# Expert stage of a two-block transformer layer: two experts side by side in the gate/up products, the sums read straight from the banks, gathers ahead in quarters, 13 ring slots

## The chip, the cores and the metric

The kernel runs on one core of a Trainium2 chip. The metric is the time of one execution on the device in microseconds (us), here as the median of several runs. The engines are named as in the profile: PE (TensorE, matrix products; PEld is its weight load), DVE (VectorE), ACT (ScalarE), POOL (GpSimd) and SP (SyncE, which here issues nearly all transfers). They run side by side and wait for one another by semaphores.

## What is computed

The reference is two transformer blocks one after the other on 512 tokens of width 1024, all in float32: a first block with a gated linear recurrence, attention and a dense feed-forward part, then a second one with three attention branches and a feed-forward part of 16 experts. The change touches the last part only:

```python
def expert_choice_ffn(x, w_router, w_gate_up, w_down):     # x (1, 512, 1024)
    cap = EC_CAPACITY_FACTOR * T // N_EXPERTS              # 64 tokens for each of 16 experts
    aff = jax.nn.softmax(x @ w_router, axis=-1)
    gate, idx = lax.top_k(jnp.swapaxes(aff, 1, 2), cap)
    xs = x[bidx, idx]                                      # (16, 64, 1024)
    h = jnp.einsum('becd,edf->becf', xs, w_gate_up)        # (16, 64, 2048)
    hg, hu = jnp.split(h, 2, axis=-1)
    ye = jnp.einsum('becf,efd->becd', jax.nn.silu(hg) * hu, w_down)
    ye = ye * gate[..., None]
    return jnp.zeros_like(x).at[bidx, idx].add(ye)
# then: layer_norm(DN_ALPHA * x + ffn, ln2_g, ln2_b)
```

The gate/up weights of an expert are 1024 x 2048 numbers (8.4 MB), its down weights 1024 x 1024 (4.2 MB), 201 MB for all sixteen. Each is used once.

## The kernel before

Everything ahead of the expert stage is a list of steps (`plan`) that each engine walks through in its own program; it is the same before and after and ends at about 1133 us. Then come `experts_sp`, `experts_pool`, `experts_act`, `experts_dve` and `experts_pe`, one function for each engine. They compute router logits, softmax and the 64 best tokens of each expert (to about 1158 us), and from there on the experts.

**Order.** Experts go in fours (`QUADS`). An item of `todo` is `("G", x)`, the gate/up products of expert x, or `("D", g)`, the down products of the pair g (experts 2g and 2g+1). The order of one quad is D of the quad before, G, G, G, D, G; in the last one it is D5, G12, G13, G14, G15, D6, D7. Every item has 8 chunks of weights, 1 MB each (128 partitions x 8 KB), 192 in all. A chunk of G holds 128 of the 1024 rows of the expert's gate/up matrix; in D, even and odd chunks belong to the two experts of the pair.

**Ring.** SP loads the chunks in order (`load`, L724). 11 tiles RING of 8 KB per partition are reused in turn (`RS`, L132). Five chunks (5, 6, 7, 13, 14) go to tiles ONCE in two halves, and those tiles aren't used again for weights. So 16 chunks are loaded ahead. Each later load waits (`slot_free`, L748) until PE has counted the chunk that held the slot as used; PE counts two chunks after each pair (`used`, L1190).

**Gate/up** (`gate_up`, L1178). The 64 tokens of an expert fill only half of the 128 columns of PE's array. So two products run in the two halves at once: the lower half takes the even chunk of a pair (a 128-row slice of the sum), the upper half the odd one, both of the same expert. After 8 chunks the four banks GU hold two partial sums, one in partitions 0 to 63, the other in 64 to 127. ACT copies the upper ones to LOH (L831), DVE adds them to the lower ones into GUS (L976), ACT makes Silu of the gate half into SG (L835), DVE multiplies (L980). PE may start the next expert in a bank only when DVE has added it (`ev`). `hidden` (L1146) turns the 64 x 1024 result with 8 transposes into one bank, and ACT copies it to HT.

**Down** (`down`, L1192). Here the two halves of the array take the two experts of a pair: sums in partitions 0 to 63 and 64 to 127 of the banks YB. ACT and DVE weight them and split them into a high and a low part (YHM, YLM). `scatter` (L1117) adds them to the tokens: 8 products with a 0/1 matrix SS, 3, 3 and 2 of them behind the first pairs of the item after D, and DVE adds each to X (L970).

**Gather** (`gather`, L1090). Before each quad PE forms the tokens of its four experts with 0/1 matrices OHT, 64 matmuls, into the four banks XG, two of which are gate/up banks. ACT scales them into the one tile XS (L822). The gather runs in one piece after the quad's last G; `columns` (each slot's token number and weight) and `hidden` follow at once.

**End.** During D6 and D7, `residual` and `late_scatter` (L1131, L1136) put X and the contribution of pair 6 into the banks; pair 7 follows, then the layer norm and the output. During G13 `spread_rows` (L1157) spreads the norm's gains over the partitions.

Of the kernel before, what the change touches and what calls it, by code (L numbers as in the profile page):

```python
# [33 lines left out]
RS = 11  # L34
# [51 lines left out]
def build(nc, x, w_in, w_out, w_ffn_in, w_ffn_out, mem, w_in2, w_memkv, w_branch, w_out2, w_router,  # L86
# [7 lines left out]
    def sem(name):  # L94
# [37 lines left out]
    RING = [at(f"RING{i}", kb, [P, 2048]) for i, kb in enumerate((*(R0 + 8 * i for i in range(8)), 181.5, 189.5, 16))]  # L132
    ONCE = {n: [at(f"ONCE{n}{h}", kb, [P, 1024]) for h, kb in enumerate(kbs)]
            for n, kbs in ((5, (52, 32)), (6, (36, 40)), (7, (44, 48)), (13, (56, 60)), (14, (197.5, 201.5)))}
# [45 lines left out]
    XS = at("XS", 8, [P, KT, QE, CAP])  # L180
    SS = at("SS", 24, [P, 2, S], F32R)
    HT = at("HT", 28, [P, 2, 2, KT, CAP])
    GUS = at("GUS", 36, [CAP, 4 * 512])
    LOH = at("LOH", 44, [CAP, 4 * 512])
    SG = at("SG", 52, [CAP, DFE])
    YHM = at("YHM", 56, [P, D], F32R)
    YLM = at("YLM", 197.5, [P, D], F32R)
    YH7 = at("YH7", 36, [P, D], F32R)
    YL7 = at("YL7", 40, [P, D], F32R)
    JUNK = at("JUNK", 44, [P, 4, 512])  # L190
# [488 lines left out]
    def tokens_first(st, f, bank, dst):  # L679
# [9 lines left out]
    (used, oht, ssr, gth, xsc, ev_lo, ev, su, hm, tp, hc, yh, yl, sct, acc) = (  # L689
        sem(n) for n in "used oht ssr gth xsc ev_lo ev su hm tp hc yh yl sct acc".split())  # L690
# [4 lines left out]
    HB = TR[0]  # L695
# [24 lines left out]
    def experts_sp(sp):  # L720
# [3 lines left out]
        def load(n):  # L724
            kind, x = todo[n // 8]
            c, r = n % 8, ring_place(n)
            if kind == "G":
                src = gu_v[:, 8 * x + c, :]
            else:
                src = dn_v[:, (2 * x + c % 2) * 4 + c // 2, :]  # L730
            if r is not None:
                sp.dma_start(RING[r % RS][:, :], src).then_inc(ring_in[r % RS], 16)
                return
            for h in range(2):
                if n == 5 and h:
# [38 lines left out]
    def experts_act(act, chain):  # L774
# [43 lines left out]
        def tokens(p):  # L818

            for d in range(KT):  # L820
                act.wait_ge(gth, 4 * p + d // 2 + 1)
                A(XS[:, d, :, :], XG[d // 2][:, d % 2 * 256:d % 2 * 256 + 256].rearrange(  # L822
                    "p (e c) -> p e c", e=QE), ACT.Identity, scale=LNC[:, 0, d:d + 1],
                  bias=LNC[:, 1, d:d + 1]).then_inc(xsc, 1)

        def gated(x):

            if x:
                act.wait_ge(ev, 4 * x)
# [3 lines left out]
            if x:  # L833
                act.wait_ge(tp, x)
            A(SG[:, :], GUS[:, 0:DFE], ACT.Silu).then_inc(su, 1)  # L835

        def hidden(x):

            act.wait_ge(tp, x + 1)
            if x == 0:  # L840
                wait(act, "xal", total)
            A(HT[:, x // 2 % 2, x % 2, :, :], HB[:, :].rearrange("p (f c) -> p f c", c=CAP), ACT.Copy).then_inc(hc, 1)

        tokens(0)
        for idx, (kind, x) in enumerate(todo):
            if idx == len(todo) - 1:
                act.preload_act_table_set("sqrt_and_others")
            else:
                act.wait_ge(used, 8 * idx + 8)
            if kind == "D":  # L850
                outputs(x)
                continue
            gated(x)
            if x % QE == QE - 1 and x < E - 1:
                tokens(x // QE + 1)
            if x == E - QE:
                rows_spread(0)
            hidden(x)
            if x == E - QE:
                for q in range(1, 4):  # L860
                    rows_spread(q)

# [29 lines left out]
    def experts_dve(dve, chain):  # L892
# [79 lines left out]
        def gated(x):  # L972
# [15 lines left out]
        for idx, (kind, x) in enumerate(todo):  # L988
            if kind == "G":
                gated(x)  # L990
                if x % QE == QE - 1 and x < E - 1:
                    slot_columns(x // QE + 1)
                if x % QE == 0 and x < E - QE:
                    dve.wait_ge(gth, x + 4)
                    one_hot_tokens(x // QE + 1)
# [39 lines left out]
    def experts_pe(pe):  # L1035
# [54 lines left out]
        def gather(p, evicted):  # L1090

            pe.wait_ge(oht, 2 * p + 1)
            if p:
# [1098 lines left out]
```

## Time and profile before

| | |
|---|---|
| median of 3 runs | 1653.49 us (1651.95 to 1653.94) |
| the profiled execution's own time | 1654.13 us |
| its span, first to last instruction | 1652.3 us |
| mean granted clock of PE over the span | 0.977 |
| busy over the span: PE, DVE, ACT, POOL | 94%, 42%, 32%, 8% |
| share of PE in the chain that ended last | 87% |
| weights' transfers in the expert stage, RING (1 MB each) | 123 of gate/up, 62 of down |

How it is read: the page gives busy time by engine, a strip of 40 slices of 41.3 us each, and the costliest groups of instructions by line. The other views are answers on the trace: the waits (who waited for whom, summed), the chain of waits (followed back from the last instruction to what released each step), the timeline, the groups by line and form, and windows. A line of the windows has: stretch, its length in us, busy us (and number of instructions) of PE, PEld, DVE, ACT and POOL, then the granted clock of PE (1.00 is full speed), the busy share of the DMA engines and the GB/s that they moved. Times are us from the span's start. A float32 matmul leaves two records, so 8 matmul calls are 16 records. "L1208 x32" in the chain is a run of 32 records of that line.

### The profile page before, as it was taken

To read this page: it belongs to the slowest core of one execution; us is meant where nothing else is said; L and a number is where in the kernel's file an instruction comes from. 1 tells how busy PE (TensorE), PEld (TensorE's weight loads), DVE (VectorE), ACT (ScalarE), POOL (GpSimd) and SP (SyncE) were. 2 spreads that over 40 slices of the span, in tenths; PEclk is the share of its full clock that TensorE was granted. 3 is DMA by queue.
4 is the path that set the end of the run, shared out by engine and by line. 5 is a ranking of instruction groups with operands and counts; after the bars stand their busy time and mean duration, and the time that the engine had idled before them with its cause. 6 is when DMAs were issued, how large, how long until landed. Compare 5 with 4: busy or idle time off the path is not lost.

```text
span 1652.3 us, 20133 instructions
## 1 busy us (share of the span) xinstructions
PE 1549.1 (94%) x7883; PEld 1085.7 (66%) x7883; DVE 701.3 (42%) x1053; ACT 531.7 (32%) x862; POOL 138.5 (8%) x186
## 2 busy tenths in 40 slices
PE   7999899999999999999999999996999999989996
PEld 6788668888888888887677678775535334334332
DVE  6565755343334335664435343366222322222223
ACT  5634534222222214234444433233222112112222
POOL 3000000000000001143102110002500000000001
PEclk9999899999999999999999999998999999999998
DMA  6221223333323327233112112429699999999993
GB/s 209 83 96 53 76 64 100 84 98 102 102 99 94 89 77 215 79 110 95 39 38 66 39 54 92 135 77 392 251 401 397 422 421 420 421 421 421 421 421 155
DMA packets 137067, 306.93 MB, mean 186 GB/s; under 512 B 7480, under 2 KB 97472, under 8 KB 113296
## 3 DMA queue, kind: packets, MB, share of 16 engines
q1 hardware_dynamic: 132608, 294.99, 47.7%
q0 software_dynamic: 3792, 10.15, 2.1%
q8 instruction: 66, 1.08, 0.3%
q10 hardware_dynamic: 576, 0.50, 0.1%
q14 instruction: 25, 0.20, 0.0%
HBM read 299.32 MB, written 4.56 MB: 184 GB/s over the span
## 4 chain that ended last, share of the span: by engine, by line
PE 87%; DVE 5%; DMA 3%; ACT 2%; issue 2%; SPq 0%; ACTq 0%; DVEq 0%
PE bank L1188 13%; PE bank L1965 12%; PE bank L1967 12%; PE bank L1966 12%; PE bank L1208 6%; PE bank L1973 4%; PE bank L1974 4%; PE bank L1975 4%; PE bank L2014 3%; PE bank L2115 2%; PE bank L2130 2%; DMA RING<-w_down 2%; PE bank L1984 2%; PE bank L1986 2%; PE bank L1985 2%
## 5 line engine op out<-in xcount | busy, mean ns | idle before, releaser
L1965 PE MATMUL bank<-XH,WH 128*128 128x512 f32 x768 | 303.5, 395 | 5.1 <-DVE XL L1795 2.0
L1967 PE MATMUL bank<-XH,WL 128*128 128x512 f32 x768 | 300.1, 391 | 0.0
L1966 PE MATMUL bank<-XL,WH 128*128 128x512 f32 x768 | 300.0, 391 | 0.0
L1616 DVE TENSOR_TENSOR WL<-RAW,WH 128x2048 fp32r<-128x2048 f32 (+1 forms) x90 | 191.8, 2131 | 142.4 <-ACT WH L1416 142.4
L1188 PE MATMUL bank<-RING,XS 128*64 128x512 f32 x496 | 224.9, 602 | 16.8 <-DVE GUS L976 14.2
L1189 PE MATMUL bank<-RING,XS 128*64 128x512 f32 x488 | 221.7, 603 | 0.0
L1416 ACT ACTIVATE WH<-RAW 128x2048 fp32r<-128x2048 f32 (+1 forms) x90 | 160.0, 1778 | 143.9 <-PE bank L1975 117.9
L1965 PEld LDWEIGHTS bank<-XH,WH 128*128 128x128 f32 x768 | 144.9, 189 | 38.4 <-issue 7.5
L1967 PEld LDWEIGHTS bank<-XH,WL 128*128 128x128 f32 x768 | 144.9, 189 | 30.7
L1966 PEld LDWEIGHTS bank<-XL,WH 128*128 128x128 f32 x768 | 145.0, 189 | 29.5 <-issue 0.2
L1188 PEld LDWEIGHTS bank<-RING,XS 128*64 128x64 f32 x496 | 65.2, 138 | 150.4 <-issue 144.8
L1208 PE MATMUL bank<-RING,HT 128*64 128x512 f32 x512 | 118.4, 614 | 6.4 <-DMA RING<-w_down 3.4
L976 DVE TENSOR_TENSOR GUS<-bank,LOH 64x512 f32<-64x512 f32 x64 | 39.6, 675 | 151.6 <-ACT LOH L831 151.6
L1208 PEld LDWEIGHTS bank<-RING,HT 128*64 128x64 f32 x512 | 39.3, 141 | 77.8 <-issue 77.6
L831 ACT ACTIVATE LOH<-bank 64x512 f32<-64x512 f32 x64 | 32.8, 590 | 178.7 <-PE bank L1189 178.6
L1973 PE MATMUL bank<-WH,AH 128*128 128x512 f32 x176 | 68.5, 389 | 1.0 <-issue 1.0
L1975 PE MATMUL bank<-WH,AL 128*128 128x512 f32 x176 | 68.5, 389 | 0.0
L1974 PE MATMUL bank<-WL,AH 128*128 128x512 f32 x176 | 68.5, 389 | 0.0
L1387 POOL TENSOR_SCALAR PB<-PB,ST 128x256 f32<-128x256 f32 (+1 forms) x80 | 46.7, 596 | 248.8 <-DVE ST L1741 248.5
L1631 DVE TENSOR_TENSOR FP<-bank,FG 128x512 f32<-128x512 f32 x22 | 15.2, 691 | 121.7 <-PE bank L1967 121.7
L1189 PEld LDWEIGHTS bank<-RING,XS 128*64 128x64 f32 x488 | 64.2, 138 | 0.0
L1984 PE MATMUL bank<-WH,XH 128*128 128x256 f32 x224 | 63.8, 285 | 0.2 <-ACT SE L1459 0.2
(360 smaller groups left out, 2411.4 us busy)
## 6 DMA issues: line engine op xcount, KB each, us to landing
RING<-w_gu SPq DMA_DIRECT2D x123, 1024.0 KB, 14.5
RING<-w_down SPq DMA_DIRECT2D x62, 1024.0 KB, 17.0
RAW<-w_in SPq DMA_DIRECT2D x66, 512.0 KB, 4.7
RAW<-w_ffn_in SPq DMA_DIRECT2D x44, 512.0 KB, 4.6
RAW<-w_ffn_out SPq DMA_DIRECT2D x20, 512.0 KB, 4.3
RAW<-w_out SPq DMA_DIRECT2D x16, 512.0 KB, 4.4
RAW<-w_branch SPq DMA_DIRECT2D x24, 256.0 KB, 2.9
ONCE<-w_gu SPq DMA_DIRECT2D x10, 512.0 KB, 19.7
```

The source lines that it names most:

```text
L1188: T.matmul(GU[b][0:CAP, :], XS[:, c - 1, e, :], weight(n - 1, 512 * b), start=c == 1, stop=c == 7)
L1189: ins = T.matmul(GU[b][CAP:P, :], XS[:, c, e, :], weight(n, 512 * b), start=c == 1, stop=c == 7)
L1208: ins = T.matmul(YB[g][h][e * CAP:e * CAP + CAP, :], HT[:, g % 2, e, 2 * r + k, :], weight(n - 1 + e, D * k + 512 * h), start=r == 0 and k ...
L1416: A(WH[:, u % 2, :n], RAW[:, u % 2, :n], ACT.Copy).then_inc(s["w_hi"], 1)
L1616: V.tensor_tensor(WL[:, u % 2, :n], RAW[:, u % 2, :n], WH[:, u % 2, :n].bitcast(F32), ALU.subtract).then_inc(s["w_lo"], 1)
L1965: T.matmul(bank[:, :st.nt], wh[:, k, c], hi, start=k == 0, stop=False)
L1966: T.matmul(bank[:, :st.nt], wh[:, k, c], lo, start=False, stop=False)
L1967: ins = T.matmul(bank[:, :st.nt], wl[:, k, c], hi, start=False, stop=k == st.K - 1)
L1973: T.matmul(bank[:, :], hi, wh[:, k, :], start=k == 0, stop=False)
L1974: T.matmul(bank[:, :], hi, wl[:, k, :], start=False, stop=False)
L1975: ins = T.matmul(bank[:, :], lo, wh[:, k, :], start=False, stop=k == st.K - 1)
L1984: T.matmul(o, XHs[:, k, t], wh[:, k, :], start=k == 0, stop=False)
```

## The change

Two experts of a pair now take the two halves of the array in G as well, so that an item `("G", g)` is a pair with 16 chunks, alternating between its experts, and the order is G0, G1, D0, G2, D1, ..., G7, D6, D7. Each bank then holds whole sums, of one expert in partitions 0 to 63 and of the other in 64 to 127. The copies to LOH and the adds into GUS fall away: ACT makes Silu from the gate banks (two instructions of 512 columns over 128 partitions), DVE multiplies with the up banks. `hidden` makes 8 transposes of 128 x 128 into two banks, once for a pair. The gather of quad p runs in four quarters ahead of chunks 6, 8, 10 and 12 of the item G(2p-1), through the two banks SB, into the other one of two XS tiles; `columns` goes to the end of D0, D2 and D4. `spread_rows` goes to the second half of G7. The ring has 13 slots, and three chunks (6, 11, 14) are loaded to ONCE tiles; it is 16 ahead in either case. The core of the diff:

```diff
-RS = 11
+RS = 13
-    RING = [... for i, kb in enumerate((*(R0 + 8 * i for i in range(8)), 181.5, 189.5, 16))]
+    RING = [... for i, kb in enumerate((*(R0 + 8 * i for i in range(8)), 181.5, 189.5, 197.5, 56, 16))]
-            for n, kbs in ((5, (52, 32)), (6, (36, 40)), (7, (44, 48)), (13, (56, 60)), (14, (197.5, 201.5)))}
+            for n, kbs in ((6, (36, 40)), (11, (44, 32)), (14, (48, 52)))}
...
-    todo = []
-    for p in range(QUADS):
-        a, b, c, d = (("G", QE * p + x) for x in range(QE))
-        before, here = ("D", 2 * p - 1), ("D", 2 * p)
-        todo += [before] * (p > 0) + ([a, b, c, d, here, ("D", 2 * p + 1)] if p == QUADS - 1 else [a, b, c, here, d])
-    chunks = 8 * len(todo)
+    todo = [("G", 0)]
+    for g in range(1, E // 2):
+        todo += [("G", g), ("D", g - 1)]
+    todo.append(("D", E // 2 - 1))
+    order = [(kind, g, c) for kind, g in todo for c in range(16 if kind == "G" else 8)]
+    chunks = len(order)
...
-                src = gu_v[:, 8 * x + c, :]
+                src = gu_v[:, 8 * (2 * g + c % 2) + c // 2, :]
...
-        for n in ringed[:-1]:
+        for n in ringed[:RS - 2]:
             load(n)
         wait(sp, "res", total)
-        for n in (ringed[-1], *sorted(ONCE, reverse=True)):
+        for n in (*ringed[RS - 2:], 6, 14, 11):
...
# ACT
-            for b in range(4):
-                A(LOH[:, 512 * b:512 * b + 512], GU[b][CAP:P, :], ACT.Copy).then_inc(ev_lo, 1)
-            act.wait_ge(ev, 4 * x + 2)
-            if x:
-                act.wait_ge(tp, x)
-            A(SG[:, :], GUS[:, 0:DFE], ACT.Silu).then_inc(su, 1)
+            act.wait_ge(used, 16 * g + 16 + 8 * max(g - 1, 0))
+            if g:
+                act.wait_ge(tp, 2 * g)
+            for h in range(2):
+                A(SG[:, 512 * h:512 * h + 512], GU[h][:, :], ACT.Silu).then_inc(su, 1)
...
# DVE
-            for b in range(4):
-                dve.wait_ge(ev_lo, 4 * x + b + 1)
-                V.tensor_tensor(GUS[:, 512 * b:512 * b + 512], GU[b][0:CAP, :],
-                                LOH[:, 512 * b:512 * b + 512], ALU.add).then_inc(ev, 1)
-            dve.wait_ge(su, x + 1)
-            dve.wait_ge(ev, 4 * x + 4)
-            V.tensor_tensor(SG[:, :], SG[:, :], GUS[:, DFE:], ALU.mult).then_inc(hm, 1)
+            for h in range(2):
+                dve.wait_ge(su, 2 * g + h + 1)
+                sg = SG[:, 512 * h:512 * h + 512]
+                V.tensor_tensor(sg, GU[2 + h][:, :], sg, ALU.mult).then_inc(hm, 1)
...
# PE
+            p, k, e = g // 2, c // 2, 2 * (g % 2)
             for b in range(4):
-                if c == 1 and x:
-                    pe.wait_ge(ev, 4 * (x - 1) + b + 1)
+                if c == 1 and g:
+                    if b < 2:
+                        pe.wait_ge(su, 2 * g + b - 1)
+                    else:
+                        pe.wait_ge(hm, 2 * g + b - 3)
...
-                T.matmul(GU[b][0:CAP, :], XS[:, c - 1, e, :], weight(n - 1, 512 * b), start=c == 1, stop=c == 7)
-                ins = T.matmul(GU[b][CAP:P, :], XS[:, c, e, :], weight(n, 512 * b), start=c == 1, stop=c == 7)
+                T.matmul(GU[b][0:CAP, :], XS[p % 2][:, k, e, :], weight(n - 1, 512 * b), start=k == 0, stop=k == KT - 1)
+                ins = T.matmul(GU[b][CAP:P, :], XS[p % 2][:, k, e + 1, :], weight(n, 512 * b),
+                               start=k == 0, stop=k == KT - 1)
...
+            if kind == "G" and x % 2 and x < LAST and c in (6, 8, 10, 12):
+                gather(x // 2 + 1, c // 2 - 3)
+            landed(n)
...
+                if prev and prev[0] == "G" and c == 3:
                     hidden(prev[1], 8 * scattered)
+                if kind == "D" and x % 2 == 0 and x < LAST - 1 and c == 7:
+                    pe.wait_ge(hc, 2 * x + 4)
+                    columns(x // 2 + 1, 8 * scattered)
+                if (kind, x) == ("G", LAST) and c > 8:
+                    spread_rows(c // 2 - 4)
...
-            if kind == "G" and x % QE == QE - 1 and x < E - 1:
-                gather(x // QE + 1, 4 * x + 4)
-                columns(x // QE + 1, 8 * scattered)
-                hidden(x, 8 * scattered)
-                made += 1
```

## Rows read from the trace of the kernel before

**Rows 1.** Page, part 2: GB/s moved, in 40 slices of the span.

```profile
GB/s 209 83 96 53 76 64 100 84 98 102 102 99 94 89 77 215 79 110 95 39 38 66 39 54 92 135 77 392 251 401 397 422 421 420 421 421 421 421 421 155
```

**Rows 2.** Windows of 20 us in the expert stage (columns as told above).

```profile
1160.00:1180.00 20.00, 20.00 (x117) 13.14 (x118) 0.61 (x4) 4.07 (x8) 9.23 (x5) 0.90 0.35 138
1180.00:1200.00 20.00, 18.43 (x91) 6.89 (x87) 7.94 (x7) 4.99 (x7) 13.34 (x6) 1.00 0.87 356
1200.00:1220.00 20.00, 18.50 (x89) 7.10 (x89) 5.80 (x9) 6.33 (x11) 0.00 (x0) 1.00 0.93 375
...
1260.00:1280.00 20.00, 19.16 (x89) 8.60 (x90) 1.99 (x7) 2.77 (x5) 0.00 (x0) 0.91 0.91 373
...
1460.00:1480.00 20.00, 16.78 (x74) 6.13 (x70) 4.68 (x7) 1.26 (x2) 0.00 (x0) 1.00 1.02 422
```

**Rows 3.** Waits of TensorE from 1150 us on: total us, times, longest us.

```profile
PE bank L1188 <- DVE GUS L976: 14.2, 9, 2.1
...
PE bank L1128 <- DVE X L970: 3.8, 12, 0.3
PE bank L1208 <- DMA RING<-w_down: 3.4, 3, 1.4
```

**Rows 4.** Waits of SyncE's DMA queue from 1050 us on, same columns.

```profile
SPq L732 <- PE bank L1189: 262.8, 63, 23.8
```

**Rows 5.** Timeline at the first gate/up products: start us, duration us, what.

```profile
1169.59 0.64 PE L1188 MATMUL bank<-RING,XS 128*64 128x512 f32 x1
...
1173.28 19.28 SPq L732 DMA_DIRECT2D RING<-w_gu  x8
```

**Rows 6.** The chain that ended last, expert stage: start us, us, what.

```profile
1134.27 2.61 PE bank L1042 x22
...
1217.22 6.87 PE bank L1208 x32
...
1225.28 7.02 PE bank L1208 x32
...
1251.98 0.32 PE bank L1102
...
1259.85 0.80 PE bank L1113 x8
...
1348.90 0.61 PE bank L1188
...
1354.74 0.57 PE bank L1188
...
1365.23 0.57 PE bank L1188
```

**Rows 7.** The same chain, from the last experts to the end.

```profile
1539.25 1.06 PE bank L1165 x4
...
1592.52 6.87 PE bank L1208 x32
...
1631.05 0.69 ACT YH L811
```

**Rows 8.** Windows of 2 us at the end of the weight transfers.

```profile
1618.00:1620.00 2.00, 2.00 (x11) 0.62 (x8) 0.00 (x0) 0.00 (x0) 0.00 (x0) 1.00 1.05 389
1620.00:1622.00 2.00, 2.00 (x6) 1.00 (x6) 0.00 (x0) 0.00 (x0) 0.00 (x0) 1.00 0.68 257
1622.00:1624.00 2.00, 2.00 (x12) 0.74 (x12) 0.00 (x0) 0.00 (x0) 0.00 (x0) 1.00 0.23 84
```

**Rows 9.** Windows of 8 us, for the granted clock beside the busy time.

```profile
1342.00:1350.00 8.00, 6.03 (x28) 1.98 (x26) 1.41 (x2) 1.26 (x2) 0.00 (x0) 1.00 1.01 417
1462.00:1470.00 8.00, 5.42 (x26) 2.01 (x26) 1.41 (x2) 1.26 (x2) 0.00 (x0) 1.00 1.01 419
1556.00:1564.00 8.00, 6.46 (x18) 2.21 (x20) 3.69 (x5) 3.06 (x6) 0.00 (x0) 0.57 1.02 423
```

**Rows 10.** Groups by line and form, ACT, from 1130 us on.

```profile
L831 ACT ACTIVATE LOH<-bank 64x512 f32<-64x512 f32 x64 | 32.8, 590 | 178.7 <-PE bank L1189 178.6
```

More of the change, by code:

```diff
@@ L688, in build @@
     row_ps, spread = sem("row_ps"), sem("spread")
-    (used, oht, ssr, gth, xsc, ev_lo, ev, su, hm, tp, hc, yh, yl, sct, acc) = (
-        sem(n) for n in "used oht ssr gth xsc ev_lo ev su hm tp hc yh yl sct acc".split())
+    (used, oht, ssr, gth, xsc, su, hm, tp, hc, yh, yl, sct, acc) = (
+        sem(n) for n in "used oht ssr gth xsc su hm tp hc yh yl sct acc".split())
     GU = [LIN[0], LIN[1], LIN[2], PV]
@@ L844, in experts_act @@
[L844 to L849, printed above, removed]
-            if kind == "D":
-                outputs(x)
-                continue
[L853 to L860, printed above, removed]
+                bank = (SB[d // 2 % 2] if p else XG[d // 2])[:, d % 2 * 256:d % 2 * 256 + 256]
@@ new lines, in tokens, with gated, hidden @@
+                A(XS[p % 2][:, d, :, :], bank.rearrange("p (e c) -> p e c", e=QE), ACT.Identity,
+                  scale=LNC[:, 0, d:d + 1], bias=LNC[:, 1, d:d + 1]).then_inc(xsc, 1)
+        def gated(g):
+            act.wait_ge(used, 16 * g + 16 + 8 * max(g - 1, 0))
[3 more added lines that the diff above has]
+                A(SG[:, 512 * h:512 * h + 512], GU[h][:, :], ACT.Silu).then_inc(su, 1)
+        def hidden(g):
+            if g == 0:
+                wait(act, "xal", total)
+            for i in range(2):
+                act.wait_ge(tp, 2 * g + i + 1)
+                A(HT[:, g % 2, 4 * i:4 * i + 4, :], TR[i][:, :].rearrange("p (f s) -> p f s", s=P),
+                  ACT.Copy).then_inc(hc, 1)
@@ L861, in experts_act @@
+        tokens(0, range(4))
+        for kind, g in todo:
+            if kind == "D":
+                if g == LAST:
+                    act.preload_act_table_set("sqrt_and_others")
+                else:
+                    act.wait_ge(used, 16 * g + 32 + 8 * g + 8)
+                outputs(g)
+                continue
+            if g % 2 and g < LAST:
+                tokens(g // 2 + 1, range(4))
+            if g == LAST:
+                for q in range(4):
                     rows_spread(q)
+            gated(g)
+            hidden(g)
@@ L990, in experts_dve @@
                 gated(x)
[L991 to L995, printed above, removed]
+                if x % 2 and x < LAST:
+                    slot_columns(x // 2 + 1)
+                if x % 2 == 0 and x < LAST - 1:
+                    dve.wait_ge(gth, 2 * x + 4)
+                    one_hot_tokens(x // 2 + 1)
             else:
@@ L1088, in experts_pe, with gather @@
         pe.wait_ge(s["x2l"], TT)
-        def gather(p, evicted):
-            pe.wait_ge(oht, 2 * p + 1)
-            if p:
-                pe.wait_ge(yl, 2 * (2 * p - 1))
-            for d in range(KT):
-                if p and d == 4:
-                    pe.wait_ge(ev, evicted)
-                o = XG[d // 2][:, d % 2 * 256:d % 2 * 256 + 256]
+        def gather(p, batch):
+            if batch == 0:
+                pe.wait_ge(oht, 2 * p + 1)
+                if p > 1:
+                    pe.wait_ge(yl, 2 * (2 * p - 2))
+            if p and batch >= 2:
+                pe.wait_ge(xsc, 8 * p + 2 * batch - 2)
+            for d in (2 * batch, 2 * batch + 1):
+                o = (SB[batch % 2] if p else XG[batch])[:, d % 2 * 256:d % 2 * 256 + 256]
                 for t in range(TT):
@@ L1124, in scatter @@
             if k == 1:
-                pe.wait_ge(s["colg"], min((g + 1) // 2 + 1, QUADS))
+                pe.wait_ge(s["colg"], min(g // 2 + 2, QUADS))
             if k >= 2:
@@ L1144, in late_scatter, with hidden @@
                     ins.then_inc(fsc, 1)
-        def hidden(x, scattered):
-            pe.wait_ge(hm, x + 1)
+        def hidden(g, scattered):
+            pe.wait_ge(hm, 2 * g + 2)
             if scattered:
                 pe.wait_ge(acc, scattered)
-            T.matmul(HB[:, 0:CAP], SG[:, 0:2 * P:2], ident[0:CAP, 0:CAP], start=True, stop=True)
-            for f in range(1, KT):
+            for f in range(KT):
                 c = slice(f // 2 * 2 * P + f % 2, f // 2 * 2 * P + 2 * P, 2)
-                ins = T.transpose(HB[:, CAP * f:CAP * f + CAP], SG[:, c], ident[0:CAP, 0:CAP])
-            ins.then_inc(tp, 1)
+                ins = T.transpose(TR[f // 4][:, f % 4 * P:f % 4 * P + P], SG[:, c], ident)
+                if f % 4 == 3:
+                    ins.then_inc(tp, 1)
         def spread_rows(q):
```

102 lines of the change are left out of this document (40 added, 62 removed).

## The prediction

> **What bounds the kernel now.** I read the page's row of GB/s first [rows 1]. The slices of 41.3 us from about 1200 us on stand at 397 and then at 420 to 422 GB/s for ten slices: a plateau. The change touches only the expert stage, and this is it: from slot choice (about 1158 us) to the end it streams 192 chunks of 1.0486 MB through the ring. The plateau says that the transfers, not the products, may set the pace. The windows then show where the stream is below it [rows 2]: 138, 356 and 375 GB/s in the first three windows and 373 at 1260 us, against 422 at 1460 us. In the latter, TensorE is busy 16.8 of 20 us.
>
> Next the waits. TensorE waits 14.2 us for the sums of the two bank halves, 3.8 us for residual sums, and only 3.4 us for weights [rows 3]. SyncE's queue in contrast waits 263 us for gate/up products to free a slot [rows 4]; but that costs nothing while earlier transfers are still in flight. So two resources run nearly level: a transfer stream of 192 chunks, and TensorE, a little behind it. The end shows which is late: the stream's rate falls from 389 to 257 to 84 GB/s in three windows of 2 us [rows 8], which is (389+257+84)/422 x 2 = 3.5 us of full rate after 1618, a nominal stream end of 1621.5 us. TensorE's last weight product ends 9.6 us after that, at 1631.05, where the tail begins [rows 7]. The tail (weighting, last scatter, layer norm, output) takes 1652.3 - 1631.05 = 21.2 us, and the change leaves it alone.
>
> **The unit of account.** One chunk at 422 GB/s [rows 2] is 1.0486/0.422 = 2.49 us, a pair 4.97 us. TensorE needs 6.87/2 = 3.44 us for a pair of down chunks [rows 6]. A gate/up pair has the same 8 matmul calls, and its first goes from 1169.59 to the slot's release at 1173.28 [rows 5]; I take 3.5 us for either. Other TensorE work: the hidden transposes of one expert 1225.28 - 1217.22 - 6.87 = 1.2 us; a gather 1259.85 - 1251.98 = 7.9 us; columns 0.8 us; eight scatters (1354.74 - 1348.90 - 3.5) + (1365.23 - 1354.74 - 7.0) = 5.8 us, their waits included [rows 6].
>
> **Part 1: products side by side, whole sums.** The number and shape of the gate/up matmuls stay, so their cost stays. What goes is, per expert, four ACT copies of 590 ns [rows 10], four adds on DVE, and TensorE's wait for them: 14.2 us in all [rows 3]. In their place one pair of experts waits for Silu and a multiply straight from the banks. Only after G0 does the next G follow at once: there the first Silu must finish before the banks are reused. No row shows a Silu of 512 columns from a bank; the copy of the same width is the nearest row, 0.59 us, so the wait is 0.6 us or so, and at most the present longest, 2.1 us [rows 3]. It falls into G1, where TensorE isn't late for anything. For all other g a down group of 14 us lies between. Value: 13 us of TensorE time. Queued behind ACT's new wait for 16 chunks are its weighted outputs; these come a group later, so nobody waits.
>
> **Part 2: transposes for two experts in one.** 16 x 1.2 us become 8 runs of 8 transposes, twice as wide. In this place the trace shows only narrow ones; a run lies between 1.2 us (width free) and 2.4 us (width pays fully). The nearest row of wide ones, 22 transposes of 128 x 128 in 2.61 us, has 0.12 us for each [rows 6], so I take 1.2: 10 us of TensorE saved; 0 is the other end. Their input (two Silus, two multiplies, 2 to 3 us) is asked for two pairs, 7 us, after the group's end: covered.
>
> **Part 3: gather ahead, in quarters, second XS.** 7.9 us stay, but now as four pieces of 2.0 us ahead of four pairs of an odd G. Before, gather, columns and transposes stood in a row and released no slot for 11 us.
>
> **Part 4: 13 ring slots and 3 once-used ones instead of 11 and 5.** 16 chunks are loaded ahead either way, so the stream's first pause (until 1173.28 plus about 1 us) stays. But used pairs now hand back 2,2,2,1,2,1,2,1 slots instead of 2,2,1,0,2,2,1,1. Before: five slots are back after three pairs, the stream has work until 1174.2 + 5 x 2.49 = 1186.6, and the next slots are freed by the fifth pair, at 1188.6 or later: it runs dry. After: seven slots, work until 1191.6, fifth pair done at 1187. Carried on pair by pair, (a chunk starts 1.1 us after its slot is free and its forerunner done), the new order keeps at least 1.5 us of work queued in G0 and 3.0 us in G1, its two tight places, so no dry spell.
>
> **Sum for the stream.** Lost before, against 422: 20 x (66+47+49)/422 = 7.7 us in the windows at 1180, 1200 and 1260 [rows 2]. All of it comes back: nominal end 1621.5 - 7.7 = 1613.8 us. (Flat 422 from 1174.2 on would give 1611.6; that is the early bound. The late bound is 1621.5, nothing regained.)
>
> **Is TensorE there in time?** Per 48 chunks it now needs 24 x 3.5 + 2 x 5.8 + 7.9 + 0.8 + 2 x 1.2 = 106.7 us, the stream 119.3. From 1169.6 its work up to G7 adds to some 345 us, 1515 us; the first pair of G7 can't have landed before 1174.2 + 146 x 2.49 = 1537. So TensorE catches up by the middle of the stage and then waits for weights, some 25 us in all: this is where the 23 us of parts 1 and 2 go. They bring no more than the stream lets through.
>
> **The end.** G7 needs 28 + 5.8 + 4 x 1.06 for spreading rows [rows 7] = 38.0 us against 39.8, its extras in front, so it may end 0 to 2 us late. D6 and D7 take 1631.05 - 1592.52 = 38.5 us as now [rows 7]. D6 starts when its first pair is there, the stream's end less 14 x 2.49 and plus 2 us for the spread of a landing: -32.8. So TensorE ends 5.7 to 7.7 us after the stream's nominal end. I take 7.7, as both extras lie on one side: 1613.8 + 7.7 = 1621.5, which is 9.5 us before today's 1631.05. Of this, 7.7 us are the stream's, 1.9 the lag's. The profiled execution's own time is 1654.13 (span 1652.3), 0.6 above the median; less 9.5 gives 1644.6 for it, and 1644.0 against the median. Forecast **1644.0 us**.
>
> **Rivals.** *More than forecast*: the lag shrinks to the least there is (2 us for landing, half a pair 1.7) and the stream ends at 1611.6: TensorE ends at 1615.3, total 1637.7. For it: TensorE has 13 us of slack per 48 chunks. Against: the extras sit in D6 and D7. Chance of under 1641: 0.09.
>
> *The dry spells stay*: with 2 to 3 us queued, any late release idles the stream, and gathers now stand among products. Then only the lag's 1.9 us are won: 1651.6, no change that could be told. For it: the two tight places. Against: from 1280 us on the stream has no dry spell even with 11 slots. Chance near that: 0.08; between: part of 1647.5 to 1650.2, 0.08.
>
> *Slower: the clock falls because TensorE now waits.* Before, the granted clock read 0.57 over 8 us after a stretch of small products and a wait [rows 9]: 3.4 us lost. If TensorE, waiting 1.5 us in 5, drops to 1.2 GHz again and again in G7, D6 and D7 (76.5 us of work on 79.6 us of stream, 3 us of slack), five such spells cost 17 - 3 = 14 us at the end where nothing regains them: 1658. It decides from four spells on; fewer only shrink the gain. Against it: the two stretches where TensorE already waits for weights show 6.03 and 5.42 busy us in 8, which is the duty I forecast, at a clock of 1.00 [rows 9]; and a slow TensorE is a busy one. Chance 0.07.
>
> [...]
>
> **How the numbers follow.** Forecast case 0.68 (1641 to 1647.5), more gain 0.09, between 0.08, dry spells 0.08, slower 0.07. A measurement of this kernel can tell about 0.2%, 3.3 us: faster means under 1650.2. Faster 0.85, same 0.08, slower 0.07. Range: from 1639.5 (half of the better case) to 1650.2 (the between case whole).
>
> **What would show it.** Right: the plateau from 1180 us on with no window under 415 GB/s; TensorE waiting 20 us or more for RING and almost none for banks; last weight product 8 us or less after the nominal stream end, that at 1614. Wrong: windows under 400 between 1180 and 1280, a clock under 1.00 in the last 80 us, or a TensorE that reaches G7 later than 1537.

## The result and the profile after

The changed kernel takes 1645.86 us (median of 5 runs, 1643.30 to 1646.51) against 1653.51 us: ratio 0.9948, 95% interval 0.9938 to 0.9959. That is 7.7 us or 0.5% faster. The forecast was 1644.0 us in a range of 1639.5 to 1650.2. The profiled execution took 1645.86 us, 8.3 less than the profiled one of before; its span is 1644.1 us. In the changed code the gate/up products are L1181 and L1182, the down products L1202, the loads L728.

The page's row of GB/s, which answers [rows 1]:

```profile
GB/s 210 80 100 52 78 64 87 94 102 103 97 83 102 102 77 192 81 131 79 57 26 73 45 52 77 128 103 323 285 421 421 422 421 421 421 421 421 421 421 170
```

Before, two slices at the head of the plateau read 401 and 397, and eight at 420 to 422 followed (the prediction names only the 397 and counts ten); now it stands at 421 from its first slice on. The windows of 20 us (columns as before) answer [rows 2]:

```profile
1160.00:1180.00 20.00, 20.00 (x116) 13.70 (x118) 0.99 (x5) 5.37 (x9) 8.38 (x4) 0.89 0.38 143
1180.00:1200.00 20.00, 19.21 (x92) 6.42 (x90) 1.05 (x2) 1.08 (x2) 12.77 (x7) 1.00 1.01 424
1200.00:1220.00 20.00, 20.00 (x110) 9.82 (x108) 1.44 (x3) 3.13 (x6) 0.00 (x0) 1.00 1.01 419
...
1260.00:1280.00 20.00, 19.68 (x88) 6.92 (x86) 3.27 (x5) 0.00 (x0) 0.00 (x0) 1.00 1.01 420
...
1380.00:1400.00 20.00, 16.05 (x74) 5.49 (x70) 0.00 (x0) 0.00 (x0) 0.00 (x0) 1.00 1.02 423
```

Where 356, 375 and 373 GB/s stood, there are 424, 419 and 420. The dry spells (stretches in which the stream has no free slot to fill) are gone, and in the window at 1380 us TensorE is busy only 16 of 20 us, at a granted clock of 1.00. TensorE's waits from 1150 us on (total, times, longest), which answer [rows 3]:

```profile
PE bank L1181 <- issue: 11.7, 11, 1.3
PE bank L1202 <- DMA RING<-w_down: 10.0, 12, 1.4
...
PE bank L1118 <- DVE X L963: 3.8, 12, 0.3
PE bank L1202 <- issue: 2.8, 3, 1.3
PE bank L1181 <- ACT SG L828: 0.8, 1, 0.8
PE bank L1181 <- DMA RING<-w_gu: 0.8, 3, 0.3
```

The 14.2 us of waiting for half sums are gone. One wait of 0.8 us for Silu stands in their place, the one between G0 and G1. There are now about 25 us of idle time in front of products whose weights are not there: 10.0 and 0.8 us are put down to the transfers, and 11.7 and 2.8 us to "issue", which are pieces of the same length (up to 1.3 us, where a pair of products takes 3.5 and a pair of chunks 5.0). That these last 14.5 us are waits for weights too is read from their length and place; pe_late below bears it out. Not all of it is new: the kernel before has 3.4 us put down to transfers and, in front of gate/up products, 2.5 us to "issue".

Windows of 2 us at the end of the stream, which answer [rows 8]:

```profile
1606.00:1608.00 2.00, 2.00 (x12) 0.75 (x8) 0.00 (x0) 0.00 (x0) 0.00 (x0) 1.00 1.03 430
1608.00:1610.00 2.00, 2.00 (x10) 0.70 (x12) 0.00 (x0) 0.00 (x0) 0.00 (x0) 1.00 0.98 390
1610.00:1612.00 2.00, 2.00 (x9) 0.58 (x6) 0.00 (x0) 0.00 (x0) 0.00 (x0) 1.00 1.02 383
1612.00:1614.00 2.00, 2.00 (x7) 1.14 (x6) 0.00 (x0) 0.00 (x0) 0.00 (x0) 1.00 0.96 353
1614.00:1616.00 2.00, 2.00 (x10) 0.63 (x10) 0.00 (x0) 0.00 (x0) 0.00 (x0) 1.00 0.54 208
1616.00:1618.00 2.00, 2.00 (x11) 0.50 (x7) 0.00 (x0) 0.00 (x0) 0.00 (x0) 1.00 0.10 38
```

From 1608 us on this is (390+383+353+208+38)/422 x 2 = 6.5 us of full rate, a nominal end of 1614.5 us. Counted in the same way from 1614 us on, where its rate begins to fall (416 and 382 GB/s, then the three rows of [rows 8]), the kernel before ends at 1621.2 us and not at the prediction's 1621.5. The chain that ended last, which answers [rows 7]:

```profile
1566.09 25.99 DMA RING<-w_down
1592.08 0.14 issue
1592.22 3.65 PE bank L1202 x16
1595.87 1.91 PE bank L1124 x4
1597.79 3.58 PE bank L1202 x16
...
1622.76 0.70 ACT YH L807
```

The chain runs through a transfer up to 1592.08 us, the third pair of D6. From there on TensorE doesn't wait for weights any more, and 30.5 us of its own work stand before the tail. In the kernel before this stretch is much longer. The last piece of its chain in which TensorE waits for weights is

```profile
1467.18 1.28 issue
```

and from 1468.46 us to 1631.05 the chain is TensorE and its waits for ACT and DVE (for half sums 1.5, 2.1 and 1.5 us). Some 5 us of this went to a granted clock under 1.00 (0.96, 0.95, 0.91 and 0.92 in the windows of 20 us at 1480, 1500, 1540 and 1560).

One pair of numbers serves for all comparisons below: the start of the first gate/up product and the end of the last weight product (where the chain goes on with ACT YH). For the changed kernel the first one is this line of the timeline:

```profile
1170.51 0.64 PE L1181 MATMUL bank<-RING,XS 128*64 128x512 f32 x1
```

It is 1622.76 - 1170.51 = 452.25 us, before 1631.05 - 1169.59 = 461.46 us [rows 5, 7]. The span is less suited to differences of 1 us, since the unchanged part ahead of the stage varies: in the next table the first product starts between 1168.8 and 1172.8 us in the kernels that are the same up to there.

Each of the two numbers has two parts, from the first product to the nominal end of the stream and from there to the last weight product:

| | stream | behind it | between |
|---|---|---|---|
| before | 1621.24 - 1169.59 = 451.65 | 9.8 | 461.46 |
| changed | 1614.50 - 1170.51 = 443.99 | 8.3 | 452.25 |

So of the 9.2 us that the stage has won, 7.7 are the stream's and 1.5 are won behind it.

### The profile page after: what moved, and what is told of

Same layout as the page of the kernel before. It is cut to its first block, busy times and chain, and to the rows that moved or that the text cites. A ratio compares the mean times of both kernels' runs of the same rounds, so it can differ in the third digit from the quotient of the medians.

```text
span 1644.1 us, 19797 instructions
## 1 busy us (share of the span) xinstructions
PE 1536.5 (93%) x7803; PEld 1073.3 (65%) x7803; DVE 649.7 (40%) x989; ACT 491.6 (30%) x798; POOL 137.4 (8%) x186
## 4 chain that ended last, share of the span: by engine, by line
PE 83%; DMA 8%; DVE 5%; issue 2%; ACT 2%; SPq 0%; ACTq 0%; DVEq 0%
PE bank L1955 12%; PE bank L1957 12%; PE bank L1956 12%; PE bank L1181 11%; DMA RING<-w_down 7%; PE bank L1963 4%; PE bank L1964 4%; PE bank L1965 4%; PE bank L1202 4%; PE bank L2004 3%; PE bank L2105 2%; PE bank L2120 2%; PE bank L1974 2%; PE bank L1976 2%; PE bank L1975 2%
## 5 line engine op out<-in xcount | busy, mean ns | idle before, releaser
L1181 PE MATMUL bank<-RING,XS 128*64 128x512 f32 x496 | 222.9, 596 | 13.3 <-issue 11.7
L1182 PE MATMUL bank<-RING,XS 128*64 128x512 f32 x504 | 226.9, 597 | 0.0
L1181 PEld LDWEIGHTS bank<-RING,XS 128*64 128x64 f32 x496 | 63.9, 136 | 143.5 <-issue 141.2
L1202 PE MATMUL bank<-RING,HT 128*64 128x512 f32 x512 | 115.6, 596 | 12.9 <-DMA RING<-w_down 10.0
L1202 PEld LDWEIGHTS bank<-RING,HT 128*64 128x64 f32 x512 | 37.8, 137 | 82.7 <-issue 82.4
L970 DVE TENSOR_TENSOR SG<-bank,SG 128x512 f32<-128x512 f32 x16 | 10.3, 686 | 200.1 <-ACT SG L828 200.1
L1182 PEld LDWEIGHTS bank<-RING,XS 128*64 128x64 f32 x504 | 65.0, 137 | 0.0
L1975 PE MATMUL bank<-WL,XH 128*128 128x256 f32 x224 | 63.4, 283 | 0.0
L1976 PE MATMUL bank<-WH,XL 128*128 128x256 f32 x224 | 63.4, 283 | 0.0
## 6 DMA issues: line engine op xcount, KB each, us to landing
RING<-w_down SPq DMA_DIRECT2D x62, 1024.0 KB, 25.3
```

The source lines that it names most:

```text
L1181: T.matmul(GU[b][0:CAP, :], XS[p % 2][:, k, e, :], weight(n - 1, 512 * b), start=k == 0, stop=k == KT - 1)
L1182: ins = T.matmul(GU[b][CAP:P, :], XS[p % 2][:, k, e + 1, :], weight(n, 512 * b), start=k == 0, stop=k == KT - 1)
L1202: ins = T.matmul(YB[g][h][e * CAP:e * CAP + CAP, :], HT[:, g % 2, 2 * r + k, CAP * e:CAP * e + CAP], weight(n - 1 + e, D * k + 512 * h), s ...
```

## Experiments

In this table, first and last are the two times just named, in each kernel's profiled execution. The ratio is against the kernel before, beside it on the same chip.

| kernel | first | last | between | ratio, 95% interval |
|---|---|---|---|---|
| before | 1169.59 | 1631.05 | 461.46 | |
| changed | 1170.51 | 1622.76 | 452.25 | 0.9948 [0.9938, 0.9959] |
| changed, again | 1168.83 | 1620.93 | 452.10 | 0.9955 [0.9941, 0.9968] |
| pe_late | 1171.39 | 1623.62 | 452.23 | 0.9951 [0.9937, 0.9965] |
| pe_g1 | 1169.62 | 1625.86 | 456.24 | 0.9979 [0.9970, 0.9988] |
| pe_end | 1172.50 | 1626.40 | 453.90 | 0.9974 [0.9962, 0.9986] |
| ring11 | 1170.48 | 1624.91 | 454.43 | 0.9963 [0.9950, 0.9977] |
| gather_whole | 1169.14 | 1622.31 | 453.17 | 0.9961 [0.9948, 0.9974] |
| ring_whole | 1172.78 | 1631.69 | 458.91 | 0.9981 [0.9971, 0.9992] |
| old_start | 1170.53 | 1631.92 | 461.39 | 1.0007 [0.9997, 1.0017] |
| early | 1160.17 | 1620.53 | | 0.9956 [0.9944, 0.9969] |
| early_res | 1162.70 | 1620.38 | | 0.9956 [0.9942, 0.9970] |
| warm | 1168.44 | 1620.84 | 452.40 | 0.9941 [0.9929, 0.9954] |
| warm_res | 1167.05 | 1618.38 | 451.33 | 0.9937 [0.9922, 0.9952] |

The theory is called A: the stage ends when the weight stream ends, and the gain is its dry spells. Its rival B: the gain is TensorE time.

**The changed kernel once more.**

> The changed kernel once more, beside the others of this group, as the level to which they are compared: 7.6 to 9.5 us (0.46 to 0.57%) below the kernel before. Both theories expect the same of it.

The ratio gives 7.4 us below the kernel before, a little less than the expected 7.6 to 9.5. Between first and last it is 452.10 us, 0.15 from the other execution. pe_late and warm, in which nothing should change between first and last, read 452.23 and 452.40, so differences of 0.5 us can be told. But each kernel has only one trace, and the ratios, uncertain by about 2 us, can't confirm a difference as small as 0.9 us.

**pe_late: TensorE time given back late.**

```diff
+                for _ in range({2: 1, 3: 1, 4: 2, 5: 1, 6: 1}.get(g, 0) if c == 1 else 0):
+                    T.matmul(GU[b][0:CAP, :], XS[p % 2][:, k, e, :], weight(n - 1, 512 * b), start=True, stop=True)
+                    T.matmul(GU[b][CAP:P, :], XS[p % 2][:, k, e + 1, :], weight(n, 512 * b), start=True, stop=True)
```

> The changed kernel with the first pair's matmuls of G2, G3, G5 and G6 made twice and those of G4 three times: 6 x 3.45 = 20.7 us of extra TensorE time, about as much as the whole sums saved; the result is the same. Theory A (the weight stream sets the end): 0, within 1 us; TensorE's waits for weights shrink from 25 to about 5 us. Theory B (TensorE's time is what counts): +20.7 us.

452.23 us: 20.7 us of extra work cost nothing. TensorE's waits for weights have paid for most of it:

```profile
PE bank L1205 <- DMA RING<-w_down: 4.3, 5, 1.4
...
PE bank L1184 <- issue: 1.3, 1, 1.3
PE bank L1205 <- issue: 1.1, 2, 0.8
```

With two small entries more (0.8 us each) they come to 8.3 us where there were 25.3, 17.0 us less; about 5 were expected to be left. What took up the other 3.7 us isn't shown. B is out as it stands: in the changed kernel TensorE's time in G2 to G6 is no part of the end.

**pe_g1: the same kind of work in G1.** The same lines with `{1: 2}`.

> The changed kernel with the matmuls of the first pair of G1 made three times (16 extra calls, 6.9 us of TensorE; the result is the same). Theory A: the work queued for the stream there is worth about 3 us, the rest comes through as a dry spell near 1207 us: +3.3 us. Theory B: +6.9 us.

456.24 - 452.25 = 4.0 us of 6.9, where A had 3.3 and B 6.9. The spell stands where A puts it:

```profile
1200.00:1220.00 20.00, 20.00 (x103) 9.04 (x101) 0.54 (x1) 2.10 (x4) 0.00 (x0) 1.00 0.88 359
1220.00:1240.00 20.00, 20.00 (x112) 10.11 (x110) 0.00 (x0) 3.06 (x6) 0.00 (x0) 1.00 1.01 412
1240.00:1260.00 20.00, 20.00 (x100) 7.71 (x98) 2.15 (x7) 3.44 (x6) 0.00 (x0) 1.00 0.99 409
```

Lost against 422: 63 + 10 + 13 = 86, times 20/422 = 4.1 us, which is the 4.0 measured. A microsecond of TensorE costs nothing in G4, and in G1 it costs one as soon as the queued transfers, 6.9 - 4.0 = 2.9 us of them, are used up.

**pe_end: extra work after the last wait.**

```diff
+                for e in range(2 if (g, c) == (LAST, 1) else 0):
+                    T.matmul(YB[g][h][e * CAP:e * CAP + CAP, :], HT[:, g % 2, 0, CAP * e:CAP * e + CAP],
+                             weight(n - 1 + e, 512 * h), start=True, stop=True)
```

> The changed kernel with 4 extra matmul calls (1.7 us) in the first pair of D7. From the third pair of D6 on TensorE waits for no weights, so theory A (the stream, and behind it the last 30 us of TensorE work) expects the whole 1.7 us at the end. The rival, that only the stream counts up to the last chunk, expects 0.

453.90 - 452.25 = 1.65 us: the whole 1.7. The end of the stage is both, the stream up to the third pair of D6 and then TensorE. So a part of B holds: behind the last wait for weights TensorE's time counts in full.

**ring11: the old ring under the new order.**

```diff
-RS = 13
+RS = 11
-    RING = [... 181.5, 189.5, 197.5, 56, 16))]
+    RING = [... 181.5, 189.5, 16))]
-            for n, kbs in ((6, (36, 40)), (11, (44, 32)), (14, (48, 52)))}
+            for n, kbs in ((5, (52, 32)), (6, (36, 40)), (7, (44, 48)), (13, (56, 60)), (14, (197.5, 201.5)))}
...
```

> The changed kernel with the old ring: 11 slots and the five once-used chunks 5, 6, 7, 13, 14. Theory A (the stage ends when the weight stream ends, and the gain is the dry spells of the stream): used pairs hand back 2,2,1,0,2,... slots again, so the stream runs dry once in G0, near 1188 us, for 1.5 us or a little more, and all of it arrives at the end: +1.5 to +3 us against the changed kernel. Theory B (the gain is the 23 us of TensorE time that the whole sums free, the ring's size does nothing): 0.

The ring's depth and the places of the once-used chunks, and with them the order of the hand-back, change together here. 454.43 - 452.25 = 2.2 us, within A's figure. The spell is between 1185 and 1190 us, as the windows of 5 us show:

```profile
1180.00:1185.00 5.00, 5.00 (x26) 1.71 (x24) 0.00 (x0) 0.00 (x0) 4.92 (x3) 1.00 1.01 428
1185.00:1190.00 5.00, 5.00 (x26) 1.73 (x24) 0.00 (x0) 0.00 (x0) 4.85 (x3) 1.00 0.80 298
1190.00:1195.00 5.00, 5.00 (x28) 1.60 (x24) 0.00 (x0) 0.00 (x0) 2.88 (x2) 1.00 1.02 433
```

It loses 124 x 5/422 = 1.5 us. The rest is in two shallow dips, 411 and 408 GB/s in the windows of 20 us from 1200 on.

**gather_whole: the gather in one piece.**

```diff
-            if kind == "G" and x % 2 and x < LAST and c in (6, 8, 10, 12):
-                gather(x // 2 + 1, c // 2 - 3)
+            if kind == "G" and x % 2 and x < LAST and c == 6:
+                for batch in range(4):
+                    gather(x // 2 + 1, batch)
```

> The changed kernel with each gather in one piece ahead of chunk 6 of G1, G3 and G5, in place of four quarters. Theory A: only the first one hurts, since later TensorE waits for weights anyway and all slots are in flight: in G1 no slot comes back for some 13 us, the stream is dry for 2.5 us near 1222 us, total +2.5 us. Theory B (TensorE's time is what counts): three times about 1 us of waiting for the banks of the third quarter, +3 us, with no dry spell in the stream.

453.17 - 452.25 = 0.9 us, where A had 2.5: the direction is right, the size isn't. The window from 1220 us reads 406 GB/s, a loss of 0.8 us. The step that failed is the length of the stretch without a hand-back. It was put at 13 us, one pair and a gather with waits for banks. In the trace the gather goes from 1209.38 us to the next product at 1217.23, 7.9 us without a wait for a bank, 11.3 us with the pair: 1.7 us less than expected, and the spell is less by as much.

**ring_whole: both together.** The edits of the last two.

> The changed kernel with the old ring (11 slots, five once-used chunks) and the whole gather at once. Alone the two cost 2.3 and 1.0 us from the first to the last weight product (452.2 us in the changed kernel, 461.5 before). If dry spells of the stream add up plainly: +3.3 us. Theory A, with the slots carried on pair by pair: the smaller ring leaves less queued when the gather stops the hand-back, the second spell grows from 2.5 to 5.9 us, together +5 to +7.5 us. Theory B (TensorE's time): +1.

458.91 - 452.25 = 6.7 us, twice the sum of the two alone (2.2 + 0.9), as A says and plain addition doesn't (B had 1 us):

```profile
1180.00:1200.00 20.00, 20.00 (x96) 6.65 (x92) 0.00 (x0) 0.00 (x0) 14.96 (x8) 1.00 0.95 396
1200.00:1220.00 20.00, 19.21 (x118) 11.72 (x115) 2.49 (x4) 5.15 (x10) 0.00 (x0) 1.00 1.00 408
1220.00:1240.00 20.00, 20.00 (x98) 7.25 (x99) 1.07 (x2) 2.19 (x5) 0.00 (x0) 1.00 0.81 325
```

The three windows lose (26+14+97) x 20/422 = 6.5 us, the one of the gather 4.6 in place of 0.8. A's account of it: two fewer slots are two fewer transfers queued when the gather stops the hand-back, so the cushion that hid most of it is gone. The queue itself was not measured.

**old_start: both, and 3.45 us of TensorE in G1.** The edits of ring_whole, and the repeated pair with `{1: 1}`.

> The same with the first pair of G1 made twice, 3.45 us of TensorE, which is about what the kernel before spent in its first four experts on waits for the half sums and on extra transposes. Theory A: all of this gain lies in how slots come back in the first 80 us, so this kernel, with the whole sums and all their saved TensorE time from G2 on, should need about as long from first to last weight product as the kernel before: +7 to +11 us against 452.2, where before is at 461.5. Theory B: the 20 us saved later stay saved, so +4 us at most.

461.39 us between first and last, against 461.46 in the kernel before, and a ratio of 1.0007. The time is that of the kernel before, though this kernel keeps the whole sums, their shorter TensorE time from G2 on and the new order:

```profile
1180.00:1200.00 20.00, 19.21 (x92) 6.40 (x90) 1.04 (x2) 1.08 (x2) 12.79 (x7) 1.00 0.97 396
1200.00:1220.00 20.00, 20.00 (x118) 11.40 (x115) 1.45 (x3) 3.13 (x6) 0.00 (x0) 1.00 0.86 355
1220.00:1240.00 20.00, 20.00 (x102) 8.00 (x102) 0.00 (x0) 2.55 (x6) 0.00 (x0) 1.00 0.79 325
```

The loss is (26+67+97) x 20/422 = 9.0 us, all in the first 70 us of products. So slots that come back late there can cost as much as the whole gain. That it comes out at the same total is partly chance, since the parts differ: the nominal end of the stream is 1623.5 us, 453.0 behind the first product (before: 451.65), and the last weight product follows 8.4 us later (before: 9.8). The stream takes 1.3 us longer than in the kernel before, and the part behind it is still as short as in the changed kernel. Nor are the spells the same ones. The kernel before lost 5.4 us up to 1220 and 2.3 us behind its second gather. Its windows of 2 us there:

```profile
1264.00:1266.00 2.00, 2.00 (x8) 0.75 (x6) 0.00 (x0) 0.00 (x0) 0.00 (x0) 0.50 1.03 430
1266.00:1268.00 2.00, 2.00 (x12) 0.82 (x10) 0.00 (x0) 0.00 (x0) 0.00 (x0) 0.90 0.58 242
1268.00:1270.00 2.00, 2.00 (x13) 0.72 (x10) 0.00 (x0) 0.00 (x0) 0.00 (x0) 1.00 0.43 90
```

These rows show something that the prediction has no term for: behind gather, columns and transposes the granted clock was at 0.50 for some 3 us, so the first pair that gave slots back was slow as well. The changed kernel reads 1.00 in every window of the stage from 1180 us on. How much of the 2.3 us the clock had isn't shown. The last step, 2.5 us for 3.45 us of TensorE, is the price of that time with the old ring; that it is the whole sums' share in the gain rests on the expectation's estimate of 3.45 us. All these runs keep the rest of the change; the kernel before itself was not run with 13 slots or with its gather split.

**early and early_res: slots back sooner.**

```diff
-    XG = [SB[0], SB[1], GU[2], GU[3]]
+    XG = [SB[0], SB[1], TR[0], TR[1]]
...
-                if c == 1 and g == 0 and b == 2:
-                    pe.wait_ge(xsc, 8)
...
-        for batch in range(4):
-            gather(0, batch)
-        columns(0, 0)
+        gather(0, 0)
...
+            if n in (2, 4, 6):
+                gather(0, n // 2)
+            if n == 8:
+                pe.wait_ge(xsc, 8)
+                columns(0, 0)
```

early_res also has `residual(0)` at `c == 1` and `residual(2)` at `c == 5` of D6.

> The changed kernel with the gather of the first quad interleaved: its quarters go through SB and TR banks instead of two gate/up banks, the first pair of G0 follows the first quarter, the others stand ahead of pairs 2, 3 and 4, columns ahead of pair 5. Theory A: the first slot comes back 6 to 7 us earlier, the stream restarts as much earlier, loses 3 to 4 us of it to short dry spells in G0, and the end comes 3.4 us earlier than in the changed kernel. Theory B: TensorE's work is the same and begins no earlier: 0.

> The kernel with the interleaved first gather, and two residual products of D6 moved two pairs ahead (from pairs 3 and 4 to pairs 1 and 3), into time in which TensorE waits for weights. Theory A: some 0.8 us less than that kernel, 4.2 us less than the changed kernel, and 12 us (0.7%) less than before. Theory B: 0 against the changed kernel.

A's figures failed, 3.4 and 4.2 us, and the result is near B's 0. The ratios are 0.9956 for both, no better than the changed kernel. Counted from the first one-hot instruction on DVE, where the choice of tokens is done (1159.09 us in the changed kernel, 1154.83 in early, 1157.36 in early_res), the last weight product ends 463.7, 465.7 and 463.0 us later. The first slot did come back early (SyncE's first load after the pause is issued at 1166.39 us in early_res against 1174.21), but then, in windows of 5 us of early_res:

```profile
1165.00:1170.00 5.00, 5.00 (x32) 2.81 (x30) 0.00 (x0) 1.02 (x2) 0.00 (x0) 1.00 0.47 170
1170.00:1175.00 5.00, 5.00 (x32) 2.76 (x30) 0.00 (x0) 0.81 (x2) 0.00 (x0) 1.00 0.88 356
1175.00:1180.00 5.00, 5.00 (x32) 2.88 (x30) 0.00 (x0) 0.33 (x2) 0.00 (x0) 1.00 0.93 362
1180.00:1185.00 5.00, 5.00 (x28) 2.17 (x26) 0.49 (x4) 2.18 (x3) 0.00 (x0) 1.00 0.98 387
1185.00:1190.00 5.00, 5.00 (x27) 1.60 (x24) 0.12 (x1) 0.00 (x0) 4.54 (x3) 1.00 0.64 234
```

With slots coming back a pair at a time the stream runs at 356 to 387 GB/s, and at 234 in the 5 us from 1185 on, which A would put down to the pair that gives back one slot only. Summed over windows of 1 us from the one-hot instruction on, early_res has moved 8.7 MB after 30 us and the changed kernel 7.1, a head start of 3.9 us; after 60 us it is 20.0 and 19.7 MB, 0.8 us. TensorE hands back 13 slots in G0 in either order and ends G0 no earlier (G1 starts 1199.09 - 1157.36 = 41.7 us after the one-hot instruction, in the changed kernel 1198.99 - 1159.09 = 39.9). The step that failed is the loss behind the early restart, put at 3 to 4 us: of a restart 6.1 us earlier (9.0 us behind the one-hot instruction in place of 15.1) only 0.8 are left after 60 us, so it is 5.3. That TensorE's work up to the end of G0 sets the pace there is my reading; no run tests it. early ends 2 us later than the changed kernel. Its gather and first pair ran at a granted clock of 0.50 and 0.55 until 1165 us, and the first pair took 5.8 us (1160.17 to the load at 1165.97) in place of 3.7, which would account for it.

**warm and warm_res: TensorE kept busy ahead of the gather.**

```diff
+        for _ in range(10):
+            T.matmul(TR[0][:, 0:256], ident, CST[:, 0:256], start=True, stop=True)
         pe.wait_ge(s["top"], 1)
...
+        for _ in range(3):
+            T.matmul(TR[0][:, 0:256], ident, CST[:, 0:256], start=True, stop=True)
         pe.wait_ge(s["x2l"], TT)
```

> The changed kernel with 10 and 3 extra matmuls of 128x256 on TensorE while it waits for the choice of tokens (their result is not used). In the traces the granted clock reads 0.50 there (the lower level) and the first gather runs at it for its first 5 us. Theory A: the stage is set by when the first product pairs hand slots back, so what makes the first gather faster moves everything: with the clock high from its start the gather takes 7.7 instead of 11 us, and the end comes 3 us earlier than in the changed kernel. The rival: the stream's own start or TensorE's catching up swallows it, 0.

> That kernel with the two residual products of D6 moved into time in which TensorE waits for weights. Theory A: the two add up, 3 us from the start and 0.8 us from the end: 3.8 us below the changed kernel and 12 us (0.7%) below the kernel before. If the start's gain is swallowed: 0.8 us below the changed kernel.

From the one-hot instruction to the first product it is 10.7 us in warm (1157.72 to 1168.44) and 10.4 in warm_res (1156.64 to 1167.05), against 11.4 in the changed kernel: 0.7 and 1.0 us, not 3. What is won there is carried through to the end (452.40 us follow, as in the changed kernel). Windows of the changed kernel, then of warm, then of warm_res:

```profile
1155.00:1160.00 5.00, 2.24 (x10) 2.06 (x10) 2.59 (x9) 0.00 (x0) 0.39 (x1) 0.50 1.03 411
1160.00:1165.00 5.00, 5.00 (x26) 5.00 (x27) 0.38 (x1) 1.02 (x2) 0.00 (x0) 0.56 0.53 211
```

```profile
1150.00:1155.00 5.00, 2.92 (x11) 2.12 (x9) 4.72 (x13) 0.00 (x0) 4.92 (x3) 0.89 1.00 419
1155.00:1160.00 5.00, 4.17 (x22) 3.62 (x23) 2.50 (x8) 0.00 (x0) 0.00 (x0) 0.80 1.03 410
1160.00:1165.00 5.00, 5.00 (x38) 5.00 (x38) 0.00 (x0) 2.04 (x4) 0.00 (x0) 0.86 0.43 172
```

```profile
1155.00:1160.00 5.00, 5.00 (x24) 4.50 (x25) 1.81 (x4) 0.00 (x0) 0.00 (x0) 0.66 1.01 404
1160.00:1165.00 5.00, 5.00 (x44) 5.00 (x43) 0.00 (x0) 2.60 (x6) 0.00 (x0) 1.00 0.05 20
```

In warm the clock stood at 1.00 through a wait of 2.4 us for the threshold and fell at 1158 us, as the gather began; its first 2.7 us ran at 0.50. In warm_res it fell at 1152 us, in a wait of 5.2 us, and was up again from 1158.5 on, so the gather ran at full clock: 8.0 us from its first product to the columns (1158.17 to 1166.16). Still only 1.0 us was won, because the 3 us of the expectation were mis-sized. In the changed kernel the gather takes 9.7 us (1159.92 to 1169.62); the 11 us counted the wait for the one-hot matrices and the columns too. So 1.7 us could be won, and the three extra matmuls put the gather's start off by 0.7 (1.53 us behind the one-hot instruction in place of 0.83). The moved residual products are worth 452.25 - 451.33 = 0.9 us, as expected. warm_res has the lowest median of all, 1642.69 us against 1653.92 for the kernel before beside it (ratio 0.9937). Its lead over the changed kernel shows in the traces (1 + 0.9 us) but is within the intervals of the ratios.

## Why the prediction was right, point by point

**The bound and the dry spells.** Right in the stream: the three windows lost 7.7 us before and 0.1 after, and the nominal stream end was 1614.5 us for a forecast of 1613.8. The difference is no more than the 0.9 us by which this execution's stage starts later (1170.51 for 1169.59 us). What the prediction left out is that the last 160 us of the stage before were TensorE's and not the stream's, and that the granted clock fell just ahead of the dry spell in the window at 1260 us.

**Whose doing they are.** The sum had put the TensorE time of parts 1 and 2 down as worthless, since TensorE waits later. For G2 to G6, pe_late shows just that. The sentence that TensorE isn't late for anything in G1 is wrong: there the same microsecond delays a slot (pe_g1: 4.0 us of 6.9), and 3.45 us of it are worth 2.5 us once the ring is short (ring_whole to old_start). The prediction missed nothing in the total by this, since it counted all lost stream time as regained. But it gave the ring and the split gather credit for 7.7 us; taken out of the changed kernel they cost 6.7 us together, and 2.2 and 0.9 alone.

**TensorE's waits for weights.** Forecast some 25 us, measured 25.3 with the pieces put down to "issue", 10.8 by the transfers that the profile names. One sign of being wrong did show: TensorE reaches G7 at 1542.5 us, not by 1537. It isn't late; it waited 1.3 us in front of this product and of three of the four pairs of D5. The 1537 was too early a bound, since it took full rate from 1174.2 us on. **The transposes.** A run of eight wide ones was taken at 1.2 us; the new kernel's groups by line show that width is free:

```profile
L1143 PE MATMUL bank<-CST,SG 128*128 128x128 f32 x64 | 9.8, 296 | 0.0
```

64 of them are busy 9.8 us, eight in 1.2 us. **The wait for Silu after G0**: forecast 0.6 us, measured 0.8.

**The end.** Forecast lag behind the stream's end 7.7 us, measured 1622.76 - 1614.5 = 8.3 us, just over the 8 that the prediction had set as its own sign. So 1.5 us are won here (from 9.8), for 1.9 forecast. This part is TensorE's: in the kernel before nothing else stands in the chain behind 1468 us. Which of the saved work has it, half sums, transposes or the clock, no run tells. The point from which TensorE no longer waits is the third pair of D6 and not the first; 30.5 us of work stand behind it, while the stream's nominal end is only 22.4 us away. pe_end and warm_res confirm that this stretch counts in full, for 1.65 and 0.9 us.

**The total.** In the stage itself 461.46 - 452.25 = 9.2 us were won, for a forecast of 9.5. The profiled executions differ by 8.3 and the medians by 7.7 us, since the unchanged part ahead of the stage came out longer in this execution, by 0.9 us at the first product. With the medians it can't be told how much of the missing 1.8 us is that part and how much is the spread of the runs (3.2 us in the changed kernel).

**The slower rival.** The clock didn't fall: the windows in which TensorE waits 4 of 20 us read 1.00, as [rows 9] had it. The 3.4 us for one spell at 0.57 were too much: the products from 1557.54 to 1563.45 us took 5.9 us where 3.0 are usual, 2.9 lost. The Trainium skill ("TensorE: Matmul & The Clock Gate", section "HAM oscillation — how this bites in real kernels") describes a kernel whose products start cold at every slice of weights, with about 2 us of products between waits of 3 to 5 us. The waits here are shorter, 1.3 us between products of 3.5 us, and the trace shows no cold start at them.

## What to carry to other kernels

Where a stream and an engine run nearly level, look for the windows in which the stream is below its plateau, and count what comes back from those. Here time freed on the engine counted in two places: where it brought a slot back that the stream was short of (G1), and behind the engine's last wait for weights (D6, D7). Between them (G2 to G6) it only became waiting. A ring's depth, the order in which its slots come back and the longest stretch of consumer work that frees none drew on one cushion here, so their effects didn't add, and each tested alone looked small (2.2 and 0.9 us here, 6.7 together). And to see differences of 1 us in a kernel of 1650, compare two fixed instructions around the changed stage, not the spans.

## What was not expected of the hardware

Where each pair of slots was refilled only as it came back (early_res, 1170 to 1185 us), the stream read 356 to 387 GB/s at a DMA share of 0.88 to 0.98, against 419 to 424 at 1.01 to 1.02 with slots in hand: this stream lost speed before it ran dry. The granted clock could fall without a long idle stretch: in the kernel before it went to 0.50 at 1263 us, behind columns and narrow transposes of some 2.2 us and a wait of 0.8. And the ten extra matmuls of warm brought it up only after 5 us of running (0.50 to 1151 us, 1.00 from 1152 on); it fell again at 1158 us, behind the wait of 2.4 us, a row of small products and three matmuls more.
